# Running sums of the gates' logarithms: two single-pass products of a high and a low part with ones, in place of one product in full precision

## What is computed

```
g = -exp(a_log) * softplus(a + dt_bias)
g = cumsum(g)                                  # within a chunk
diff = g[..., :, None] - g[..., None, :]
decay = where(lower, exp(where(lower, diff, 0.0)), 0.0)
A = where(strict, einsum('bhid,bhjd->bhij', kb, kc) * decay, 0.0)
```

## Time and profile before

| | us |
|---|---|
| median of 3 runs (lowest to highest) | 1041.63 (1041.61 to 1042.81) |
| the profiled execution's own time | 1040.92 |
| its span, first to last instruction | 1039.1 |
| PE busy | 1024.7 (99% of the span) |
| DVE, ACT, POOL busy | 741.5, 606.9, 212.3 |
| mixer of layer 0, about 212 to 335 us: PE, DVE, ACT, POOL busy of 123.00 | 122.70, 99.46, 76.89, 14.32 |

### The profile page before, as it was taken

One profiled execution on the slowest core, in us unless ns is written; L12 is line 12 of the kernel. 1 busy time (PEld: TensorE's weight loads), 2 busy tenths in 40 slices (PEclk: granted clock), 3 DMA queues, 4 the chain that ended last, 5 costly groups with the idle time before them and its releaser, 6 DMA issues.

```text
span 1039.1 us, 18922 instructions
## 1 busy us (share of the span) xinstructions
PE 1024.7 (99%) x6464; PEld 886.3 (85%) x6464; DVE 741.5 (71%) x1201; ACT 606.9 (58%) x1070; POOL 212.3 (20%) x253
## 2 busy tenths in 40 slices
PE   7999999999999999999999999999999999999997
PEld 6888888899987888888888888889989888888885
DVE  5777666799776766666686666668986876666665
ACT  6555555787555655555675555558774556555554
POOL 3755111100400221111122111110014003111111
PEclk9999999999999999999999999999999999999999
DMA  8866666585124576666647666665731238666661
GB/s 260 263 190 188 188 185 191 143 240 154 62 62 122 163 211 192 183 188 195 183 133 217 194 183 183 193 172 161 223 102 63 82 101 245 200 183 188 192 185 41
DMA packets 249882, 176.79 MB, mean 170 GB/s; under 512 B 5876, under 2 KB 235401, under 8 KB 249705
## 3 DMA queue, kind: packets, MB, share of 16 engines
q1 hardware_dynamic: 248800, 174.35, 56.7%
q0 software_dynamic: 400, 1.43, 0.4%
q10 hardware_dynamic: 632, 0.34, 0.1%
HBM read 175.05 MB, written 1.05 MB: 169 GB/s over the span
## 4 chain that ended last, share of the span: by engine, by line
PE 94%; DVE 2%; ACT 1%; POOL 1%; issue 1%; DVEq 0%; POOLq 0%; ACTq 0%
PE bank L737 29%; PE bank L740 15%; PE bank L721 13%; PE bank L722 13%; PE bank L723 13%; PE bank L746 1%; PE bank L781 1%; PE bank L1109 1%; PE bank L1122 1%; DVE xr L2044 1%; PE bank L1042 1%; PE bank L995 1%; DVE Wl L1828 0%; PE bank L788 0%; PE bank L1024 0%
## 5 line engine op out<-in xcount | busy, mean ns | idle before, releaser
L1828 DVE TENSOR_TENSOR Wl<-raw,Wh 128x1024 fp32r<-128x1024 f32 x324 | 417.9, 1298 | 78.7 <-ACT Wh L1374 78.6
L1374 ACT ACTIVATE Wh<-raw 128x1024 fp32r<-128x1024 f32 x324 | 331.7, 1054 | 82.8 <-PE bank L723 82.2
L737 PE MATMUL bank<-X,Wh 128*128 128x512 f32 x1344 | 336.8, 393 | 0.0
L737 PEld LDWEIGHTS bank<-X,Wh 128*128 128x128 f32 x1344 | 246.7, 188 | 49.0
L740 PEld LDWEIGHTS bank<-X,Wl 128*128 128x128 f32 x1344 | 182.8, 189 | 14.7 <-DVE Wl L1828 0.9
L616 POOL TENSOR_TENSOR gact<-gact,pooled 128x256 f32<-128x256 f32 x88 | 77.6, 882 | 569.5 <-DVE gact L1922 432.4
L740 PE MATMUL bank<-X,Wl 128*128 128x256 f32 x1344 | 187.4, 282 | 0.0
L721 PE MATMUL bank<-Wh,aH 128*128 128x512 f32 x336 | 132.8, 395 | 1.4 <-DVE aL L1943 1.3
L722 PE MATMUL bank<-Wl,aH 128*128 128x512 f32 x336 | 131.8, 392 | 0.0
L723 PE MATMUL bank<-Wh,aL 128*128 128x512 f32 x336 | 131.5, 392 | 0.0
L1480 ACT ACTIVATE dec<-bank 128x256 f32<-128x256 f32 x88 | 33.6, 382 | 125.0 <-PE bank L740 124.9
(11 more groups left out here) (308 smaller groups left out, 1290.2 us busy)
## 6 DMA issues: line engine op xcount, KB each, us to landing
raw<-in_ffn_w_gate SPq DMA_DIRECT2D x88, 512.0 KB, 4.0
raw<-in_ffn_w_up SPq DMA_DIRECT2D x88, 512.0 KB, 3.7
raw<-in_ffn_w_down SPq DMA_DIRECT2D x88, 512.0 KB, 4.4
raw<-in_w_in SPq DMA_DIRECT2D x48, 512.0 KB, 4.6
raw<-in_w_out SPq DMA_DIRECT2D x16, 512.0 KB, 3.3
cst<-in_consts POOLq DMA_DIRECT2D x1, 1200.0 KB, 8.4
xr<-in_x SPq DMA_DIRECT2D x2, 512.0 KB, 4.3
out_x<-big SPq DMA_DIRECT2D x3, 256.0 KB, 2.1
```

Of the source, the lines that this page charges most:

```text
L737: nc.tensor.matmul(b[:, :], piece(Wh, s)[:, k, :], X[:, k, :, :], start=k == 0, stop=False)
L1374: return nc.scalar.activation(Wh[:, s, 0:D_MODEL], raw[:, s, :], ACT.Copy).then_inc(hi_cast.sem, 1)
L1828: return nc.vector.tensor_tensor(Wl[:, s, 0:D_MODEL], raw[:, s, :], Wh[:, s, 0:D_MODEL].bitcast(F32), ALU.subtract).then_inc(lo_cast.sem, 1)
```

## The change

The product with ones is no longer made in full precision. A matrix of ones of type fp32r (`ones_r`) is made once at the start by POOL, between the memsets and the select. DVE makes two further small steps after the fifteenth: a high part of the 8 log decays, rounded to fp32r by a copy, and a low part, the difference. POOL scales the triangle twice, once by each part, into two fp32r tiles that lie where `LT` and `aT` lie. PE multiplies `ones_r` by both for each half, accumulating in the bank: four products of 128x512 instead of two. PE's wait on `gstep` goes from 15 to 17 and its wait on `tri_g` from 1 to 2; the waits on `ident_made` go from 3 to 4.

```diff
--- before.py
+++ after.py
@@ -214,6 +214,7 @@
         trig = sb("trig", [P, 2, HALVES, ATT_DIM])
         sind, cosd = trig[:, 0, :, :], trig[:, 1, :, :]
         diag = sb("diag", [P, HALVES, P])
+        ones_r = sb("ones_r", [P, P], F32R)
 
         QK = sb("QK", [P, DN_HEADS, 2, SEQ])
         VT = sb("VT", [P, DN_HEADS, SEQ])
@@ -262,6 +263,8 @@
         nrm_first = hid[0:DEPTH * KT, 1, 0:P]
         nrm_rest = hid[2 * DEPTH * KT:4 * DEPTH * KT, 1, 0:P]
         O, Vn = grow, LT
+        g_hi, g_lo = ga[:, 9, 8:16].bitcast(F32R), ga[:, 10, 8:16].bitcast(F32R)
+        grow_parts = [X0[:, 2 * i:2 * i + 2, :, :].rearrange("p k a (u t) -> p (k a u) t", t=P) for i in range(2)]
 
         def weights_of(h):
 
@@ -377,10 +380,10 @@
         gate_hi = signal("gate_hi", 1)
         gate_lo = signal("gate_lo", 1)
         gates_in = signal("gates_in", 2)
-        gstep = signal("gstep", 15)
+        gstep = signal("gstep", 17)
         gexp = signal("gexp", 1)
         gln = signal("gln", 1)
-        tri_g = signal("tri_g", 1)
+        tri_g = signal("tri_g", 2)
         cum_col = signal("cum_col", 1)
         cum_row = signal("cum_row", 2)
         cum_read = signal("cum_read", 1)
@@ -555,6 +558,7 @@
             made(nc.gpsimd.memset(ident, 0.0))
             made(nc.gpsimd.memset(ones, 1.0))
             pool.wait_ge(ident_made.sem, 2)
+            made(nc.gpsimd.tensor_copy(ones_r[:, :], ones))
             made(nc.gpsimd.affine_select(out=ident.unsqueeze(1), in_=ident.unsqueeze(1), compare_op=ALU.not_equal, fill=one,
                                          base=0, pattern=[[0, 1], [-1, P]], channel_multiplier=1))
 
@@ -658,10 +662,11 @@
                 pool.wait_ge(*att_in.at(layer, ATT_EARLY))
                 nc.gpsimd.memset(DT[:, :, 0:HALF], 0.0).then_inc(cleared.sem, 1)
 
-                pool.wait_ge(*gstep.at(layer, 15))
-                nc.gpsimd.tensor_tensor(grow[:, :, :], tri.unsqueeze(1).broadcast_to([P, UNITS, P]),
-                                        ga[:, 9, 0:8].unsqueeze(2).broadcast_to([P, UNITS, P]),
-                                        ALU.mult).then_inc(tri_g.sem, 1)
+                pool.wait_ge(*gstep.at(layer, 17))
+                for to, g in zip(grow_parts, (g_hi, g_lo)):
+                    nc.gpsimd.tensor_tensor(to, tri.unsqueeze(1).broadcast_to([P, UNITS, P]),
+                                            g.bitcast(F32).unsqueeze(2).broadcast_to([P, UNITS, P]),
+                                            ALU.mult).then_inc(tri_g.sem, 1)
 
                 for c in range(HALVES):
                     pool.wait_ge(*lt_raw.at(layer, 2 * c + 2))
@@ -815,7 +820,7 @@
 
                 n = 2 * f
                 if layer == 0 and f == 0:
-                    pe.wait_ge(ident_made.sem, 3)
+                    pe.wait_ge(ident_made.sem, 4)
                     for _ in range(WARM):
                         nc.tensor.matmul(bank[7][:, 0:2 * P], ident, cst[:, C_IDENT:C_FIRST], start=True, stop=True)
                     for c, b in ROW_ORDER:
@@ -1013,16 +1018,18 @@
 
                 z_piece(0)
 
-                pe.wait_ge(*gstep.at(layer, 15))
+                pe.wait_ge(*gstep.at(layer, 17))
                 pe.wait_ge(*convd.at(layer, 9))
                 nc.tensor.matmul(bank[1][:, 0:UNITS], tri, ga[:, 9, 0:UNITS], start=True,
                                  stop=True).then_inc(cum_col.sem, 1)
-                pe.wait_ge(*tri_g.at(layer, 1))
+                pe.wait_ge(*tri_g.at(layer, 2))
                 pe.wait_ge(*convd.at(layer, 10))
                 pe.wait_ge(*ln2.at(layer, 1))
                 for c in range(HALVES):
-                    nc.tensor.matmul(bank[2 + c][:, :], ones, grow[:, 4 * c:4 * c + 4, :], start=True,
-                                     stop=True).then_inc(cum_row.sem, 1)
+                    for i in range(2):
+                        m = nc.tensor.matmul(bank[2 + c][:, :], ones_r[:, :], grow_parts[i][:, 4 * c:4 * c + 4, :], start=i == 0,
+                                             stop=i == 1)
+                    m.then_inc(cum_row.sem, 1)
                 z_piece(1)
 
                 for n in range(4):
@@ -2128,6 +2135,8 @@
 
                 small(nc.vector.scalar_tensor_tensor(ga[:, 1, 0:8], ga[:, 1, 0:8], 0.0, ga[:, 11, 0:8], ALU.max, ALU.add))
                 small(nc.vector.scalar_tensor_tensor(row(9), row(1), -1.0, per_head(19), ALU.mult, ALU.mult))
+                small(nc.vector.tensor_copy(g_hi, ga[:, 9, 0:8]))
+                small(nc.vector.tensor_tensor(g_lo, ga[:, 9, 0:8], g_hi.bitcast(F32), ALU.subtract))
                 beta, gc, eg, neg_e = ga[:, 7, :], ga[:, 16, :], ga[:, 17, :], ga[:, 18, :]
                 lo_mix(layer, 21)
 
@@ -2335,7 +2344,7 @@
             dve.sem_inc(x_new.sem, 4)
             nc.vector.memset(bias[:, 0:1], EPS).then_inc(zeroed.sem, 1)
             dve.wait_ge(zeroed.sem, 1)
-            dve.wait_ge(ident_made.sem, 3)
+            dve.wait_ge(ident_made.sem, 4)
 
             def mixer_casts(layer):
                 return lambda j: lo_mix(layer, j)
```

## The result

The changed kernel takes 1044.72 us (median of 11 runs, 1044.04 to 1047.25), the kernel before beside it 1042.63 (11 runs, 1041.42 to 1043.74). The ratio is 1.0022, 95% interval 1.0014 to 1.0030: some 2.3 us slower. The forecast was +2.4, to 1044.0, with a range up to 1045.8.

A forecast was written before the change was run, and what follows sets the result against it. PE was taken to bound the kernel, with short margins on the other engines. Two layers of 1.1 us lateness plus 0.2 at the start gave +2.4 us on the median 1041.63, so 1044.0, range 1041.0 to 1045.8.

The forecast's parts named there:

- PE's saving: Product with ones on PE: four single-pass products replace four full-precision records, saving 0.85 us each layer.
- s: DVE's lateness at conv_rest(10), from the added small steps and POOL's second product; put at 2.3 us.
- s - 1.21: Lateness of level_d at level 0, reached through ACT's value copies; forecast 1.1 us each layer.
- POOL and DVE exclude one another: DVE instructions with two SBUF inputs and POOL's products can't overlap, so the second product costs DVE its length, 1.90 us.
- the second case: Behind the small steps DVE's cast goes first, one norm falls between POOL's two products; s about 2.4 us.
- The two smaller waits: PE waiting 0.7 us before the value transposes for ACT's SiLU, and level_p 0.5 us late behind DVE's unit_gram.
- s - 2.5: Lateness of PE's value transposes behind ACT's last SiLU: not later than before, but eating PE's saving.
- s - 1.8: Lateness of level_p at level 0, waiting for DVE's first transposed half; 0.5 us, inside level_d's 1.1.
- POOL's product with fp32r output: Price of each scaled triangle on POOL: 1.90 us as with f32 output, 2.3 kept for the upper end.
- Rival 3: fp32r costs more on POOL, 2.3 us each product: s 3.1, +4.0 us, 1045.6; chance 0.12.
- Rivals 1, 2 and 4: Little waits, 1040.1 (0.10); DVE goes on while POOL waits, 1041.3 (0.16); product with ones not single-pass, 1045.4 (0.02).
- The start: POOL's copy of the ones before the select delays PE's first products: 0.2 us, bounds 0 and 0.3.

The follow-up runs named there:

- one POOL product: Changed kernel with only the high-part POOL product, read by all four PE products (low part left out, timing only); ratio 0.9986.
- before, second at half width: Kernel before plus a second POOL product of triangle and log decays, half as wide (128x512), which PE waits for; ratio 0.9999.
- before, two: Kernel before plus a second full-width f32 POOL product of triangle and log decays, which PE waits for; ratio 1.0014.
- before, three: Kernel before plus two additional 128x1024 POOL products, PE waiting for two of the three; ratio 1.0049.
- the reordered one: Changed kernel with ACT's value copies ahead of the high casts 24 to 26 and the third gate's SiLU; ratio 1.0001.
- the copy moved: Changed kernel with POOL's copy of the ones moved behind the identity's select at the start; ratio 1.0025.
- a change of order on two queues: Changed kernel with conv_rest(10) right behind DVE's small steps and ACT's value copies ahead of casts, 0.9992; with cast 24 put back ahead, 0.9990.
- ACT's order alone: Kernel before with only ACT's value copies moved ahead of the three high casts and third gate's SiLU; ratio 1.0004.

## Why the prediction was right, step by step

The margins, read before, against what the traces gave (us, each layer; the last column takes two layers and nothing else; where PE's saving isn't in the kernel, 0 stands for -0.79):

| kernel | s | max(-0.79, s - 1.21) | level_d late | ratio measured | ratio from it |
|---|---|---|---|---|---|
| one POOL product | 0.30 | -0.79 | -0.79 | 0.9986 | 0.9985 |
| before, second at half width | 0.84 | (0) | 0.01 | 0.9999 | 1.0000 |
| before, two | 1.69 | 0.48 | 0.46 | 1.0014 | 1.0009 |
| changed | 2.01 | 0.80 | 0.79 | 1.0022 | 1.0015 |
| before, three | 3.41 | 2.20 | 2.18 | 1.0049 | 1.0042 |

- **PE's saving.** Forecast 0.85, measured 0.79.
- **POOL and DVE exclude one another.** Shown: the norms held at 2.12, and all of it gone with the second product. The order that I took as the second case came, the cast first; its s was put at 2.4 and is 2.0. What I missed: 0.23 us of the cast's own wait for ACT swallowed half of the two small steps, and each norm was held 1.7 us, not POOL's whole 1.9. The rule of the Trainium skill, "SBUF — State Buffer", section "SBUF: two separate sides", agrees with both rows of 2.12.
- **The way to PE.** s - 1.21 for level_d was right to 0.02 in the three kernels in which it sets PE's time; the two others lie on the other side of the margin and lose nothing, as the rule has it. That ACT's queue carries it is shown by the reordered one. The two smaller waits came as named. The value transposes wait 0.2 (forecast 0.7 with s at 2.3): they are 22.27 behind the first small step, before 22.72, so s - 2.5 = -0.49 against -0.45. level_p waits 0.45 and comes 0.13 late, where s - 1.8 gives 0.21.
- **POOL's product with fp32r output.** The two took 4.97 us, with a wait for the cast of about 1.2 in the first. One by one they are 2.94 and 2.07, and two such products with f32 output, in the kernel with three, 2.88 and 2.08: the fp32r output costs nothing more, as forecast. Rival 3 is out. So is the estimate of 2.2 us from the Trainium skill, "GPSIMD Engine Reference", section "Elementwise — side-by-side cycle accounting": the product that nothing held, in the kernel before, took 1.90. Rivals 1, 2 and 4 are out by the rows above.
- **The start.** Forecast +0.2. Not seen; it is less than the start's own variation.
- **What the sum lacked** is, by the profiles, the granted clock. The waits give 2 x 0.79 = 1.6 us, not 2.2 + 0.2. Of the measured 2.3 some 0.7 is left. The same count, the measured difference less PE's lateness in both layers, leaves 0.7 to 1.1 us in each of the four measurements whose profile has the clock fall behind PE's waits (the changed kernel twice, the copy moved, three POOL products), and -0.6 to +0.5 in the nine others, where it didn't fall. One ratio has 0.8 us or more on either side, so the 0.7 alone is within noise: the clock is its likely source, not a shown one. The sum was right to 0.1 us by luck: s too large by 0.3 and the start counted, against what was left out.

How often the clock falls isn't settled. It fell in one mixer of two in each of three profiles with all three waits (and in one of two with three POOL products), which for 1.5 us each would make +3.1 and not +2.3. In none of the 20 mixers of the other ten profiles did it fall, those with a single wait of 0.3 to 0.4 us and the one with two of 0.2 and 0.45 among them. That the waits bring it about is inferred from this, and from the 0.8 us, within noise, that the reordered kernel gained beyond its waits; no run changed the clock alone.

## What to carry to other kernels

Idle time of POOL isn't free while DVE works on two inputs in SBUF: price a POOL product by what it holds of the DVE queue (here 1.6 to 1.7 us of each 1.9), and put DVE work that reads PSUM beside it (here 1.5 us, not held). Where PE is the bound, list for each other engine the margin until PE waits; a saving on PE moves PE towards those margins from one side, while the added work moves them from the other. Here 0.8 us saved met 2.0 us of lateness against a margin of 1.21, and a change of order on two queues gave the saving back. On the kernel before, ACT's order alone gave nothing.

## What the runs showed that I had not expected

- The granted clock went to 0.50 for about 3 us behind three waits of PE of 1.2 us in sum, and cost 1.5 us, about as much as level_d's lateness in both layers together. It is seen as a step in the distance of like products (0.64 for three instead of 0.36) while PE is counted as fully busy.
- Products with new weights for every 128 columns take about 0.12 us each in one pass, as much as a record of a full-precision product: sixteen take 1.8 to 1.9 us in both forms.
- The time from the start to the first mixer's gates varied from 247.2 to 249.9 us between profiles of kernels that are the same there but for the copy of the ones, more than the whole effect of the change.
